# A decoder layer whose two middle token blocks leave gathering for dense products over all experts, while VectorE gathers the first and last block

## What is computed

```python
q = (xt @ w_query).reshape(T, PEER_HEADS, 2, PEER_D_HALF)
s = jnp.einsum('thcd,hckd->thck', q, sub_keys)
top_s, top_i = lax.top_k(s, PEER_TOPK)                 # 16 of 128, twice per head
best_s, pos = lax.top_k(cand_s, PEER_TOPK)             # 16 of the 256 sums
expert_idx = jnp.take_along_axis(cand_i, pos, axis=-1) # 8 heads x 16 = 128 per token
gate = jax.nn.softmax(best_s, axis=-1)
u = jnp.take(expert_u, ic, axis=0)
h = gelu(jnp.einsum('cd,ced->ce', xc, u))
vv = jnp.take(expert_v, ic, axis=0)
out = jnp.einsum('ce,ced->cd', gc * h, vv)
```

## Time and profile before

| | |
|---|---|
| time, median of 3 executions | 1658.43 us (1653.55 to 1658.89) |
| span of the profiled execution, first to last instruction | 1633.5 us |
| median less that span (start and end outside it) | 24.9 us |
| busy PE, DVE, ACT, POOL | 1276.5, 1155.6, 267.2, 625.2 us |
| moved by DMA | 603.44 MB, of which gathered 536.91 MB |
| granted TensorE clock, mean | 0.896 |

### The profile page before, as it was taken

How to read it: one execution, slowest core, us unless ns; L and a number is a source line. 1 busy time by engine, 2 the same in 40 slices (tenths; PEclk the granted TensorE clock), 3 DMA queues, 4 the chain that set the end, 5 groups by cost and what they waited for, 6 DMA issues and landing times.

```text
span 1633.5 us, 11511 instructions
## 1 busy us (share of the span) xinstructions
PE 1276.5 (78%) x3448; PEld 618.1 (38%) x3448; DVE 1155.6 (71%) x2727; ACT 267.2 (16%) x754; POOL 625.2 (38%) x645
## 2 busy tenths in 40 slices
PE   7879979888646994586978687878777878787885
PEld 5465446433323562232323233333333333332332
DVE  1349999767798979987676767776767677764454
ACT  0110000121211111121212121212121212121111
POOL 0004344474445565543434343434342434343320
PEclk9989999999767997798888888989897989899899
DMA  9939798897759898999999999999999999999993
GB/s 339 390 140 353 280 344 312 319 409 274 263 189 335 319 373 329 410 422 421 422 421 421 422 422 421 422 421 422 421 422 421 422 421 422 421 422 421 421 422 127
DMA packets 125710, 603.44 MB, mean 369 GB/s; under 512 B 12624, under 2 KB 14928, under 8 KB 76368
## 3 DMA queue, kind: packets, MB, share of 16 engines
q0 software_dynamic: 92160, 536.91, 81.2%
q1 hardware_dynamic: 33488, 65.80, 11.0%
HBM read 600.57 MB, written 2.10 MB: 369 GB/s over the span
## 4 chain that ended last, share of the span: by engine, by line
DMA 38%; PE 31%; DVE 23%; issue 3%; POOL 2%; SPq 1%; ACT 1%; DVEq 0%; POOLq 0%
DMA arena<-uv,idx 37%; PE W L474 7%; PE W L509 7%; DVE arena L1060 5%; PE ACC L474 4%; DVE xs L1052 4%; PE W L744 3%; PE W L716 3%; PE ACC L461 2%; POOL arena L438 2%; PE W L515 2%; DVE arena L1039 1%; DMA arena<-w_in 1%; DVE cand L1301 1%; DVE cand L1303 1%
## 5 line engine op out<-in xcount | busy, mean ns | idle before, releaser
L474 PE MATMUL W<-arena,fdiag 128*128 128x512 f32 x1024 | 498.9, 648 | 170.1 <-ACT fdiag L979 170.1
L426 POOL DMA_INDIRECT arena<-uv,idx x384 | 367.5, 957 | 586.7 <-PE W L474 355.7
L1060 DVE SCALAR_TENSOR_TENSOR arena<-arena,X 128x1024 f32<-128x1024 f32 x256 | 309.2, 1219 | 200.8 <-DMA arena<-uv,idx 199.7
L438 POOL DMA_INDIRECT arena<-uv,idx x256 | 257.3, 1005 | 372.2 <-DVE idx L1311 125.1
L474 PEld LDWEIGHTS W<-arena,fdiag 128*128 128x128 f32 x1024 | 208.6, 208 | 459.7 <-issue 253.0
L474 PE MATMUL ACC<-arena,fdiag 128*128 128x512 f32 x512 | 254.9, 660 | 69.3 <-ACT fdiag L979 69.3
L1060 DVE SCALAR_TENSOR_TENSOR arena<-arena,W 128x1024 f32<-128x1024 f32 x128 | 154.8, 1219 | 95.8 <-DMA arena<-uv,idx 95.4
L474 PEld LDWEIGHTS ACC<-arena,fdiag 128*128 128x128 f32 x512 | 107.0, 213 | 217.2 <-issue 132.1
L979 ACT ACTIVATE fdiag<-ident,gate 128x128 f32<-128x128 f32 x384 | 123.3, 390 | 354.7 <-DVE gate L1067 351.0
L1039 DVE SCALAR_TENSOR_TENSOR arena<-arena,X 128x1024 f32<-128x1024 f32 x128 | 150.0, 1216 | 24.8 <-DMA arena<-uv,idx 24.3
L509 PE MATMUL W<-arena 128*128 128x512 f32 x320 | 143.7, 605 | 9.7 <-DMA arena<-w_in 9.0
(11 more groups left out here) (178 smaller groups left out, 824.7 us busy)
## 6 DMA issues: line engine op xcount, KB each, us to landing
arena<-w_in SPq DMA_DIRECT2D x13, 2048.0 KB, 13.8
arena<-peer_w_query SPq DMA_DIRECT2D x8, 2048.0 KB, 14.4
arena<-uv,idx POOLq DMA_INDIRECT x640, 25.4
arena<-w_out SPq DMA_DIRECT2D x4, 2048.0 KB, 14.9
arena<-w_in SPq DMA_DIRECT2D x4, 512.0 KB, 6.4
out<-xs SPq DMA_DIRECT2D x4, 512.0 KB, 8.1
arena<-xT SPq DMA_DIRECT2D x1, 1536.0 KB, 18.2
xs<-x SPq DMA_DIRECT2D x1, 1536.0 KB, 17.0
```

The lines of the kernel that those rows point to most:

```text
L426: pool.indirect_dma_start(out=fused[slot], out_offset=None, in_=uv, in_offset=bass.IndirectOffsetOnAxis(ap=idx[:, E + n:E + n + 1], axis=0 ...
L438: pool.indirect_dma_start(out=ring[:, r, :], out_offset=None, in_=rows, in_offset=bass.IndirectOffsetOnAxis(ap=idx[:, e:e + 1], axis=0), e ...
L474: last = nc.tensor.matmul(sum_of(b)[:, half * HW:(half + 1) * HW], fdiag[:, n % ND, :], fused[n % NS][:, D + half * HW:D + (half + 1) * HW ...
L1060: STT(out=fused[slot][:, 0:D], in0=fused[slot][:, 0:D], scalar=1.0, in1=token_of(b), op0=ALU.mult, op1=ALU.mult, accum_out=hid[:, E + n:E ...
```

## The change

Which rows are gathered, and by whom:

- Blocks 1 and 2 (256 tokens) gather nothing. For each of 128 *tiles* of 128 experts, PE multiplies the tile of U (streamed from `uT`, 0.5 MB) with the 256 tokens (`up`: 8 matmuls of 256 columns), ACT takes the Gelu (`hidden`), DVE multiplies with the gate matrix (`mask_hidden`, 256 columns), and PE adds the product with the tile of V (`add`: 4 matmuls of 512 columns). 56 hidden tiles fit at a time.
- The gate matrix (16384 experts by 256 tokens, zero but for the picks) is made by products of one-hot matrices: DVE writes 8 tensors of 128 columns for four tokens (`hot_quads`), PE multiplies them (`quad`), ACT copies them out (`take_quad`) and sends them to memory in 8 pieces of 2 MB; SP brings them back in 16 pieces of 1 MB (`load_g`).
- Blocks 0 and 3 gather single rows, 512 in all, through the ring of 8; DVE does every dot (L1052) and every addition (L1070). `rows(n)` now counts single rows.
- In wave 1 `rows(2)` and `rows(4)` stand where `rows(1)` and `rows(2)` (4 and 8 rows) stood; no row within the three attentions; 7 rows behind each retrieval unit of block 1 and the later ones of block 2.
- Block 3's four retrieval units run in pieces beside the tiles 2 to 13. SP's loads (`load_u`, `load_v`) are 0.5 MB each, into rings of four; rows and tiles of U and V alike are pieces of 4 KB per partition.
- `gn` and `lam_in` share memory with other things, and an unused PSUM copy of the tokens is gone.

```diff
+GATHERED = [0, 3]
+DENSE = [1, 2]
+NT = P
+NH = 56
+LEAD = 8
+TAIL = 4
+UP_FIRST = NH - ND * QUADS // 4
...
+            for n in range(UR, NH + UR):
+                load_u(n)
+            for i in range(2):
+                sp.wait_ge(spill_landed[i], 16 * (NC // 2))
+            load_g(0)
+            for n in range(VR):
+                load_v(n)
...
+            def up(n):
+                pe.wait_ge(u_landed[n % UR], 16 * (n // UR + 1))
+                if n >= 2:
+                    pe.wait_ge(h_ready, n - 1)
+                for k in range(KD):
+                    last = nc.tensor.matmul(h_bank(n), u_ring[n % UR][:, k, :], actT[:, k, P:P + TD],
+                                            start=(k == 0), stop=(k == KD - 1))
...
-            attend(1, [[0], [1], [2], [3]])
-            add_rows(4)
...
-                add_pairs(b)
+            for n in range(UP_FIRST):
+                up(n)
+            for d in range(ND):
+                turn_picks(d)
+                for q in range(d * QUADS, (d + 1) * QUADS):
+                    quad(q)
+                    if q % 4 == 3:
+                        up(UP_FIRST + q // 4)
+            pe.wait_ge(quad_taken, ND * QUADS)
+            for n in range(NT - TAIL):
+                pe.wait_ge(masked, n + 1)
+                pe.wait_ge(v_landed[n % VR], 16 * (n // VR + 1))
+                for d in range(ND):
+                    last = add(n, d)
+                last.then_inc(v_done, 1)
+                if n + NH < NT:
+                    up(n + NH)
...
+            for n in range(UP_FIRST):
+                hidden(n)
+            for d in range(ND):
+                take_picks(d)
+                for q in range(d * QUADS, (d + 1) * QUADS):
+                    take_quad(q)
+                    if q % 4 == 3:
+                        hidden(UP_FIRST + q // 4)
...
+                    for m in range(4):
+                        t = 4 * (q % QUADS) + m
+                        TS(b_hot[:, q % OH_RING, m, :], iota_f[:], pT[d % 2][:, 1, t:t + 1], None, ALU.is_equal)
+                        last = TS(a_hot[:, q % OH_RING, m, :], iota_f[:], pT[d % 2][:, 0, t:t + 1],
+                                  pT[d % 2][:, 2, t:t + 1], ALU.is_equal, ALU.mult)
...
+            rows(8)
             ln1(3)
+            rows(12)
+            for s in range(4):
+                retrieve(1, s)
+                rows(7)
+            best_keys(2, 0)
+            norm_picks(0)
+            best_pairs()
+            best_experts(2, 0)
+            hot_quads(0)
+            for s in range(1, 4):
+                retrieve(2, s)
+                rows(7)
+            norm_picks(1)
+            rows(E - taken[0])
+            hot_quads(1)
+            weigh(0)
+            for n in range(LEAD):
+                mask_hidden(n)
+            for n in range(NT):
+                if n + LEAD < NT:
+                    mask_hidden(n + LEAD)
+                if 2 <= n < 14:
+                    s, stage_of = divmod(n - 2, 3)
+                    if stage_of == 0:
+                        best_keys(3, s)
...
+                if taken[0] == 3 * E and n < 66:
+                    pass
+                else:
+                    if n == 66:
+                        weigh(1)
+                    rows(min(4, 3 * E - taken[0]) if n < 66 else 3)
...
```

More of the change, by code:

```diff
@@ L54 @@
 RING = 8
[L55 to L69, removed]
-NS = 18
[L71 to L77, removed]
+QUARTER = E // 4
+GATHERED = [0, 3]
+DENSE = [1, 2]
+ROWS = 2 * E * len(GATHERED)
+ND = len(DENSE)
+TD = ND * P
+NT = P
+NH = 56
+NS = 18
+UR = 4
+VR = 4
+LEAD = 8
+TAIL = 4
+QUADS = P // 4
+OH_RING = 4
+OH_BANKS = 5
+CHUNK = 32
+NC = TD // CHUNK
+PER_CHUNK = CHUNK // 4
+GT = 8
+UP_FIRST = NH - ND * QUADS // 4
 RQ, RK, RV, RG, DQ, DKK, DV = range(7)
@@ L445, in _ @@
-            pairs(EARLY, NF)
+            pool.wait_ge(query_ready, WQ)
+            for s in range(ROWS):
+                g, e = s // (2 * E), s % E
+                col = g * E + e
+                is_u = s // E % 2 == 0
+                if is_u and e % QUARTER == 0:
+                    pool.wait_ge(experts_ready, 4 * GATHERED[g] + e // QUARTER + 1)
+                if s >= RING:
+                    pool.wait_ge(row_used[s % RING], s // RING)
+                pool.indirect_dma_start(
+                    out=ring[:, s % RING, :], out_offset=None, in_=rows,
+                    in_offset=bass.IndirectOffsetOnAxis(ap=idx[:, col:col + 1], axis=0),
+                    element_offset=0 if is_u else D,
+                ).then_inc(row_landed[s % RING], 16)
@@ new lines, in gathered_gelu, with hidden @@
+            def gathered_gelu(g):
+                cols = slice(g * E, (g + 1) * E)
+                last_dot = g * 2 * E + E - 1
+                for i in range(RING):
+                    act.wait_ge(row_used[(last_dot - i) % RING], (last_dot - i) // RING + 1)
+                nc.scalar.activation(hid[:, cols], hid[:, cols], ACT.Gelu).then_inc(gelu_ready, 1)
+            def hidden(n):
+                act.wait_ge(u_ready, n + 1)
+                if n >= NH:
+                    act.wait_ge(v_done, n - NH + 1)
+                elif n >= 48:
+                    act.wait_ge(experts_ready, 12)
+                elif n >= 40:
+                    act.wait_ge(experts_ready, 8)
+                nc.scalar.activation(h_slot(n), h_bank(n), ACT.Gelu).then_inc(h_ready, 1)
@@ L1009, in _ @@
+            for d in range(ND):
+                take_picks(d)
[3 more added lines that the diff above has]
+                        hidden(UP_FIRST + q // 4)
+            gathered_gelu(0)
+            for n in range(NH, NT):
+                hidden(n)
+                if n == NH + 18:
+                    gate_exp(1)
+                elif n == NH + 64:
+                    gathered_gelu(1)
         @block.vector
@@ new lines, in mask_hidden, with rows @@
+            def mask_hidden(n):
+                g = n // GT
+                if n % GT == 0:
+                    dve.wait_ge(g_landed[g % 2], 16 * (g // 2 + 1))
+                dve.wait_ge(h_ready, n + 1)
+                h = h_slot(n).rearrange("p (c t) -> p c t", c=NC)
+                TT(out=h, in0=h, in1=g_ring[g % 2][:, :, n % GT * CHUNK:(n % GT + 1) * CHUNK],
+                   op=ALU.mult).then_inc(masked, 1)
+            taken = [0]
+            def rows(n):
+                for s in range(taken[0], min(taken[0] + n, ROWS)):
+                    if s // E % 2 == 0:
+                        dot(s)
+                    else:
+                        add_row(s)
+                taken[0] = min(taken[0] + n, ROWS)
@@ L1343, in _ @@
             ln1(0)
-            taken = [0]
-            def rows(n):
-                for k in range(taken[0], taken[0] + n):
-                    if k < HALVES:
-                        dots(k)
-                    else:
-                        sums(k - HALVES + ON_PE)
-                taken[0] += n
             retrieve(0, 0)
@@ L1436, in constants @@
+            for d in range(ND):
+                join_sums(d)
+                finish(DENSE[d])
 def constants():
```

526 lines of the change are left out of this document (230 added, 296 removed).

## The result

The changed kernel takes **1810.64 us** (median of 4, 1808.81 to 1811.96) against 1658.66 for the kernel before on the same chip: 1.0916 times, 95% interval 1.0893 to 1.0938. It is slower by 152 us. The forecast was 1833 (1775 to 1890); the span was forecast as 1808 and is 1809.5.

What follows compares the result with a forecast made beforehand. The prediction took gathering to bound the old kernel's second half and DMA the new loop. About 950 us before the loop, 858 from there and 24.9 outside the span made 1833 us, 10.5% slower, range 1775 to 1890.

Steps and rivals of the forecast that it cites:

- Queries at 560: Front of the kernel: the queries' last scores stored at 560 us instead of 630.2, 70 us gained.
- DVE waits some 110 us for the exponential behind 40 tiles: Behind the queries: DVE waits from about 589 us for block 1's exponential, queued behind 40 tiles up ending at 698.
- One-hots 58 us a block: Before the loop: DVE's 32 groups of one-hot tensors at 1.8 us each, 58 us for each of blocks 1 and 2.
- 28 rows in 32 to 35 us: Between later retrieval units and block 2's one-hots: DVE does 28 rows in 32 to 35 us, to 875.
- The DMA is the longest claim of a tile: Loop of 128 tiles: DMA needs 8.27 us a tile at 400 GB/s, more than PE's 6.88 or DVE's rows and mask.
- The rival at 360 GB/s: Loop: two queues reading at once get only 360 GB/s, 9.1 and 6.2 us a tile, 1899 us; chance 13%.
- the one not bound by DMA: Loop: rows and tiles arrive faster than any row shows, PE and DVE set the pace, 1678 us; chance 4%.
- The rate of 422: Rival for the loop: everything streams at 422 GB/s, 7.77 and 5.28 us a tile, 1792 us; chance 22%.
- PE's last 11 tiles and the end, 49 us: End of the kernel: PE's last 11 tiles take 38 us, then 11 from the last matmul to the last instruction.
- The sum: Whole span: about 950 us before the loop plus 858 from there to the end, 1808.
- The fourth rival: Before the loop: one-hots cost twice, gate pieces come late, loop starts at 1000 instead of 950, 1883 us; chance 6%.
- with the 24.9 outside it: Whole kernel: 24.9 us taken as time outside the span, added to 1808 to give 1833 us.

Runs made afterwards that it cites:

- e1: Changed kernel with PE and ACT doing 8 tiles up, then block 1's picks and one-hot products, then 32 tiles, then block 2's: 1742.2 us.
- e2: Changed kernel with block 0's 49 dot rows behind block 1's picks moved in front of DVE's wait for the exponential: 1743.3 us.
- e7: As e1, with the 28 rows behind DVE's second wait for an exponential moved in front of it: 1714.0 us.
- e4: Changed kernel loading only the first four tiles of V and reusing them, 65 MB less moved, output not the reference's: 1685.8 us.
- a0: The changed kernel again, unedited, beside the kernel before: 1810.5 us against 1655.9.
- e5: The kernel before with each 8 KB pair gathered as two pieces of 4 KB, same bytes: 1781.0 us against 1654.5.

## Why the forecast was right, and the term that was off

*Queries at 560.* They were at 557.07: the front gained 73 us where 70 was forecast. That wasn't luck. Taken between the same products of PE before and after, the projections gained 7.3 us for 7, block 1's attention 29.1 for 30, block 2's 22.0 for 21, and block 3's with the way to the queries' first product 15.0 for 12.

*DVE waits some 110 us for the exponential behind 40 tiles.* 113.73, ended by L980, at 697.61. e1, e2 and e7 show that it was real time in front of the loop: what came off it came off the end, within 4 us.

*One-hots 58 us a block.* 708.65 to 766, and 57 for block 2's; from start to start 0.20 and 0.25 us, as worked out from the operations on 1024 columns, against 0.26 and 0.32 for the operations on PSUM. The Trainium skill (VectorE: DVE Perf Modes, "Mode 2x_2P") gives two results a cycle to a 32-bit scalar operation whose source is in SBUF; the trace agrees with the lower cost.

*28 rows in 32 to 35 us.* They took 45.6 (837.84 to 883.4), because POOL issued one only every 1.6 us (last section), a limit that the forecast didn't have. The scores had come 3 us early and the gates took 15 as forecast, so the first mask was at 956.2 for 950.

*The DMA is the longest claim of a tile.* e4 shows it. 8.27 us were forecast for a tile at 400 GB/s, 8.0 measured at 404; the first 64 tiles took 548 us for 563. The 43 tiles behind, with the weights of block 3, took 243 for 246. The Trainium skill (DMA: Bandwidth & Descriptors, Specifications) has some 358 GB/s as one core's limit, half of what its memory gives two cores. This kernel runs on one core, and its trace goes beyond that: 402 to 408 GB/s from 1200 to 1700 us. The rival at 360 GB/s is out, and so is the one not bound by DMA. The rate of 422 wasn't reached either, though 548 us for the first 64 tiles lie between its 538 and the forecast's 563.

Two signs didn't come as said. In the loop PE was to wait for masks; it waited 17.8 us for masks and 76.3 for tiles of V, in 12 waits. DVE waited for a row 182 times in 384 there, not at nearly every one.

*PE's last 11 tiles and the end, 49 us.* 62 measured (1747.2 to 1809.5): PE still had between 12 and 13 tiles, and waited 4.56 us for a V tile in them. From PE's last product to the end it was 11.6 us for 11.

*The sum.* +6, -15, -3 and +13 cancel: 1808 forecast, 1809.5 measured. That is luck, better than its parts deserve.

*A rival's price.* The fourth rival's words and its time don't fit: one-hots at twice 58 us, for two blocks, would start the loop near 1066, not at 1000. The measured 57 a block put it out either way.

**The term that was off is "with the 24.9 outside it".** I subtracted the span of the profiled execution from the median of the runs and took the rest as time outside the span. a0 shows 2 us there. The kernel before's executions differ from chip to chip (medians 1636, 1639, 1654, 1656, 1659; the spans of the first four are 2 us below), and its profile, with 1633.5, is like the faster ones. The changed kernel gave 1810.6 and 1810.5 beside before's 1658.7 and 1655.9. All of the 22 us between 1833 and 1810.6 are this term; without it the forecast was 1810.

Not foreseen: ACT stood 50 us for block 3's last dots at L964, up to 1504, and PE 27.8 behind it. The DMA went on at 408 GB/s in that stretch, so it cost little if anything; it wasn't tried alone.

Left open: why the kernel before differs by 20 us between chips, for which there is only one trace; and what the changed kernel takes where the kernel before takes 1636.

## What to carry to other kernels

When two engines hand work to one another, look for the stretch where each waits for the other in turn: here the loop needed 790 us whenever it started, and a 0.3 us exponential queued behind 40 tiles, not the arithmetic, set when. Work for an engine should be counted against the resource that bounds the end: rows beside the attentions looked like a cost to PE and were the cheapest transfers of the kernel. And before a difference of span and median goes into a sum, ask whether both come from the same chip.

## What the runs showed of the hardware

In full slices of 5 us a gather whose pieces are 4 KB moved 407 to 420 GB/s (e5), one of 8 KB 418 to 428 (the kernel before). A mix of gathers and tiles of 4 KB on two queues moved 402 to 408 (the changed kernel, stretches of 50 to 200 us between 1200 and 1700).

POOL's issue of a gather isn't always 1.25 us from start to start. In the changed kernel's 28 rows without other loads, POOL waits for nothing that the profile shows, but its records grow to 1.99 us beside DVE's dots. Timeline of POOL, and the stretch:

```profile
838.36 1.51 POOL L443 DMA_INDIRECT arena<-uv,idx  x1 [0.30 <-issue]
840.17 1.98 POOL L443 DMA_INDIRECT arena<-uv,idx  x1 [0.30 <-issue]
842.46 1.99 POOL L443 DMA_INDIRECT arena<-uv,idx  x1 [0.30 <-issue]
844.75 0.96 POOL L443 DMA_INDIRECT arena<-uv,idx  x1 [0.30 <-issue]
...
843.00:883.00 40.00, 0.00 (x0) 0.00 (x0) 28.55 (x47) 0.00 (x0) 32.69 (x25) 0.50 0.88 305
```

24 rows are issued in 39 us, 1.6 each, and the DMA moves 305 GB/s. What stretches the records was not tried. One difference is on record: these dots read the tokens from `xs`, in SBUF (L1052), those of the kernel before from their copy in PSUM (L1060), and beside those a record of POOL took 0.96 us on average (L426).
